# Output stages of a two-layer attention trunk: inverse sums loaded from DRAM as repeated rows, and the gates multiplied with them by GpSimd

## The reference

```
o     = attention output, still to be divided by the softmax sum of its head and token
mixed = (o / sum) * silu(gate)            # for A the factor is the RMS norm's inverse root instead
x     = x + mixed @ w_out                 # 1024 x 1024
out   = x * rsqrt(mean(x*x) + eps) * g    # the next layer's input, or the result
```

## Time and profile before

| | |
|---|---|
| runs, us | 2565.64, 2559.77, 2558.90 |
| median, us | 2559.77 |
| profiled execution, us | 2567.35 |
| its span, us | 2565.5 |
| mean granted TensorE clock | 0.973 |
| PE busy in the span | 2377.9 us, 93% |
| DVE, ACT, POOL busy | 60%, 44%, 42% |

### The profile page before, as it was taken

How to read it: one execution, slowest core, us unless ns; L and a number is a source line. 1 busy time by engine, 2 the same in 40 slices (tenths; PEclk the granted TensorE clock), 3 DMA queues, 4 the chain that set the end, 5 groups by cost and what they waited for, 6 DMA issues and landing times. The chain is left out here.

```text
span 2565.5 us, 46268 instructions
## 1 busy us (share of the span) xinstructions
PE 2377.9 (93%) x17864; PEld 1976.7 (77%) x17864; DVE 1528.9 (60%) x2849; ACT 1137.0 (44%) x2401; POOL 1072.4 (42%) x852
## 2 busy tenths in 40 slices
PE   5999999997999998799879999899997999998998
PEld 4777778875888877688768888788885888887887
DVE  6444565334988897855554423744223888887555
ACT  4333343333777776622143333433332666665221
POOL 6687758772000002401068877678774201000000
PEclk9999999998999999899989999999998999999999
DMA  3555434456663234757334444345434453533452
GB/s 130 169 177 177 152 118 149 148 176 149 136 145 88 63 115 132 215 199 261 131 130 158 160 126 141 99 156 170 126 103 146 147 178 129 189 130 112 165 196 83
DMA packets 220745, 376.76 MB, mean 147 GB/s; under 512 B 54980, under 2 KB 108912, under 8 KB 219504
## 3 DMA queue, kind: packets, MB, share of 16 engines
q1 hardware_dynamic: 199376, 296.21, 36.4%
q0 software_dynamic: 19792, 75.50, 10.0%
q10 hardware_dynamic: 1360, 2.10, 0.2%
HBM read 236.33 MB, written 142.90 MB: 148 GB/s over the span
## 5 line engine op out<-in xcount | busy, mean ns | idle before, releaser
L1092 PE MATMUL p_acc<-p_operands,p_w_hi 128*128 128x512 f32 x1600 | 613.5, 394 | 5.1 <-DVE p_full_out L959 4.9
L310 POOL TENSOR_TENSOR p_w_lo<-p_w_raw,p_w_hi 128x512 fp32r<-128x512 f32 x240 | 332.8, 1395 | 153.1 <-ACT p_w_hi L573 152.8
L1092 PE MATMUL p_acc<-share,p_w_hi 128*128 128x512 f32 x1024 | 385.2, 396 | 12.5 <-DVE p_operands L735 6.1
L1092 PEld LDWEIGHTS p_acc<-p_operands,p_w_hi 128*128 128x128 f32 x1600 | 303.6, 190 | 67.1 <-POOL p_w_raw L328 4.7
L1092 PE MATMUL p_acc<-share,p_w_lo 128*128 128x512 f32 x896 | 351.2, 392 | 0.0
L573 ACT ACTIVATE p_w_hi<-p_w_raw 128x512 fp32r<-128x512 f32 x252 | 156.5, 624 | 244.8 <-POOL p_w_raw L328 113.8
L1092 PE MATMUL p_acc<-share_low,p_w_hi 128*128 128x512 f32 x624 | 250.4, 401 | 12.5 <-DVE p_operands L735 6.1
L1092 PE MATMUL p_acc<-share_low,p_w_lo 128*128 128x512 f32 x624 | 246.1, 394 | 0.0
L1092 PEld LDWEIGHTS p_acc<-share,p_w_hi 128*128 128x128 f32 x1024 | 192.8, 189 | 54.9 <-DVE p_operands L735 8.9
L865 DVE SCALAR_TENSOR_TENSOR p_lo_out<-p_full_out,p_hi_out 128x512 fp32r<-128x512 f32 x116 | 123.1, 1061 | 180.3 <-ACT p_hi_out L590 180.3
L1850 DVE CUSTOM_DVE_ANT_0 c_prob<-c_logits,c_bias 128x640 f32<-128x640 f32 (+4 forms) x256 | 179.5, 738 | 68.8 <-PE c_logits L1783 52.6
(11 more groups left out here) (285 smaller groups left out, 4743.7 us busy)
## 6 DMA issues: line engine op xcount, KB each, us to landing
scr_qh<-p_hi_out SPq DMA_DIRECT2D x116, 256.0 KB, 2.5
scr_ql<-p_lo_out SPq DMA_DIRECT2D x116, 256.0 KB, 2.8
p_w_raw<-in_w_in_even POOLq DMA_DIRECT2D x26, 1024.0 KB, 7.5
scr_gt<-p_hi_out SPq DMA_DIRECT2D x128, 128.0 KB, 2.1
ready_w<-in_w_in_odd POOLq DMA_DIRECT2D x16, 1024.0 KB, 6.9
p_w_raw<-in_w_in_odd POOLq DMA_DIRECT2D x16, 1024.0 KB, 6.9
share<-scr_qh SPq DMA_DIRECT2D x28, 512.0 KB, 8.3
share<-scr_ql SPq DMA_DIRECT2D x28, 512.0 KB, 9.6
```

What stands on the lines that cost most here:

```text
L310: nc.gpsimd.tensor_tensor(w_lo[:, k, :, :], w_source(e, k), w_hi[:, k, :, :].bitcast(F32), ALU.subtract).then_inc(w_made, 1)
L1092: last = nc.tensor.matmul(bank[:, :], wt[:, k, c, :], at[k][:, c, :], start=starts and step == 0, stop=step == 3 * HK - 1, skip_group_chec ...
```

## The change

For tiles 0 and 1 the inverses come as before; tile 0 is done in two halves of 4 feature groups each (`pieces`), so that its first matmuls need only the first half. For tiles 2 to 15 there is no widening by POOL and no transposing by PE. Instead PE transposes the whole table of inverses once (`turn_inverses`, two products into PSUM `junk`), ACT copies it to SBUF (`inv_t`), SP stores it to a DRAM scratch `scr_inv` and waits until it has landed (`store_inverses`). Then SP loads each tile's rows from there, each row of 128 tokens repeated over 64 or 128 partitions by a zero stride of the source, into `post.wide` (`load_wide`). POOL multiplies the gates with `wide` (both in SBUF) into `gated`, once `mix` of the tile before is done. The loads of tiles 2 and 3 are issued ahead of the loop; that of tile t + 3 is issued in iteration t behind the load of x. DVE keeps `mix` and `m_lo`. Semaphore targets are raised by one for tile 0's second half (`after_tile(t)` is t + 2).

```diff
+        inv_rows = scr["inv"]
+        SPREADS = 2
+        rest = post.earlier
+        invs = [(post.inv_sums, min(post.heads, P // TILES) * h, min(post.heads, P // TILES)) for h in range(post.heads * TILES // P)]
+        if rest:
+            invs.append((rms, 0, rest))
+        WIDE_LOADS = 3 if rest else 2
+        HALVES = ((0, KC // 2), (KC // 2, KC))
...
         @block.gpsimd
...
-            for t in range(2, TILES):
-                pool.wait_ge(spread_done, t - 1)
-                post.widen(t, rms)
+            for t in range(SPREADS, TILES):
+                b = t // TPB
+                pool.wait_ge(wide_loaded[t % 2], 16 * WIDE_LOADS * (t // 2))
+                if b == 0:
+                    pool.wait_ge(post.tile_loaded[t], 32)
+                elif t % TPB == 0:
+                    pool.wait_ge(blk_loaded[b % 2], 32 * ((b + 1) // 2))
+                pool.wait_ge(mixed, after_tile(t - 1))
+                nc.gpsimd.tensor_tensor(gated[:, :, :], g_sb[b % 2][:, :, t % TPB * P:(t % TPB + 1) * P], post.wide[:, t % 2, :, :], ALU.mult).then_inc(scaled, 1)
...
         @block.sync
+            def store_inverses():
+                sp.wait_ge(inv_copied, len(invs))
+                for n, (source, first, heads) in enumerate(invs):
+                    sp.dma_start(inv_rows[n * P:n * P + heads * TILES, :], inv_t[0:heads * TILES, n, :]).then_inc(inv_stored, 16)
+                sp.wait_ge(inv_stored, 16 * len(invs))
+
+            def load_wide(t):
+                if t < 2 * SPREADS:
+                    sp.wait_ge(spread_done, t - 1)
+                else:
+                    sp.wait_ge(scaled, after_tile(t - 2))
+                for r in range(2):
+                    rows = bass.AP(tensor=inv_rows.tensor, offset=inv_rows.offset + (r * TILES + t) * P, ap=[[0, HD], [2 * TILES * P, KC - rest], [1, P]])
+                    sp.dma_start(post.wide[r * HD:(r + 1) * HD, t % 2, rest:KC, :], rows).then_inc(wide_loaded[t % 2], 16)
+                if rest:
+                    rows = bass.AP(tensor=inv_rows.tensor, offset=inv_rows.offset + (P + t) * P, ap=[[0, P], [TILES * P, rest], [1, P]])
+                    sp.dma_start(post.wide[:, t % 2, 0:rest, :], rows).then_inc(wide_loaded[t % 2], 16)
...
             sp.dma_start(gain[:, :], gain_dram.partition_broadcast(P)).then_inc(gain_loaded, 16)
+            store_inverses()
+            for t in range(SPREADS, 2 * SPREADS):
+                load_wide(t)
             for t in range(TILES):
                 if t + 2 < TILES:
                     load_x(t + 2)
+                if 2 * SPREADS <= t + 3 < TILES:
+                    load_wide(t + 3)
...
         @block.scalar
+            def high(t):
                 if t >= 2:
                     act.wait_ge(mm_done, 2 * (t - 1))
+                for n, (lo, hi) in enumerate(pieces(t)):
+                    act.wait_ge(mixed, n + 1 if t == 0 else after_tile(t))
+                    nc.scalar.activation(m_hi[:, t % 2, lo:hi, :], mix[:, lo:hi, :], ACT.Copy).then_inc(hi_done, 1)
+
+            high(0)
+            for n, (source, first, heads) in enumerate(invs):
+                act.wait_ge(inv_turned, n + 1)
+                nc.scalar.activation(inv_t[0:heads * TILES, n, :], junk[0:heads * TILES, n * BLK:n * BLK + P], ACT.Copy).then_inc(inv_copied, 1)
...
         @block.vector
-                dve.wait_ge(spread_done, t + 1)
-                nc.vector.tensor_tensor(gated[:, :, :].rearrange("p c (r t) -> p c r t", t=HD), g_sb[b % 2][:, :, tokens].rearrange("p c (r t) -> p c r t", t=HD),
-                                        spread_tokens, ALU.mult).then_inc(scaled, 1)
...
+                gate(0)
+                mixture(0)
+                if t == 0:
+                    gate(1)
+                low(0)
+                if t == 0:
+                    mixture(1)
+                    low(1)
...
         @block.tensor
             def spreads(t):
                 if t >= 1:
-                    pe.wait_ge(scaled, t)
+                    pe.wait_ge(scaled, after_tile(t - 1))
...
             spreads(0)
+            turn_inverses()
             for t in range(TILES):
-                if t + 1 < TILES:
+                if t + 1 < SPREADS:
                     spreads(t + 1)
-                pe.wait_ge(lo_done, t + 1)
+                if t >= 1:
+                    pe.wait_ge(lo_done, after_tile(t))
                 for half in range(2):
...
                     for c in range(KC):
+                        if t == 0 and half == 0 and c in (0, KC // 2):
+                            pe.wait_ge(lo_done, 1 if c == 0 else 2)
```

More of the change, by code:

```diff
@@ L2152, in output @@
         gated, mix = st.sb("gated", [P, KC, P]), st.sb("mix", [P, KC, P])
+        inv_t = st.sb("inv_t", [P, 2, P])
         x_sb = st.sb("x", [P, 2, D])
@@ L2162, in output @@
         spread_done, scaled = (st.sem(x) for x in ("spread_done", "scaled"))
+        inv_turned, inv_copied, inv_stored = (st.sem(x) for x in ("inv_turned", "inv_copied", "inv_stored"))
+        wide_loaded = st.sems("wide_loaded", 2)
         gain_loaded = st.sem("gain_loaded")
@@ L2168, in output, with pieces, after_tile @@
         gt = scr["gt"].rearrange("(c p) t -> p c t", p=P)
+        inv_rows = scr["inv"]
         x_v, y_v, n_v = (None if d is None else d.rearrange("(t p) d -> t p d", p=P) for d in (x_dram, y_dram, norm_dram))
+        SPREADS = 2
[5 more added lines that the diff above has]
+        HALVES = ((0, KC // 2), (KC // 2, KC))
+        def pieces(t):
+            return HALVES if t == 0 else ((0, KC),)
+        def after_tile(t):
+            return t + 2
         block = ctx.enter_context(nc.Block())
@@ L2218, in _ @@
         def _(act):
-            def hi(t):
-                act.wait_ge(mixed, t + 1)
+            def high(t):
                 if t >= 2:
                     act.wait_ge(mm_done, 2 * (t - 1))
-                nc.scalar.activation(m_hi[:, t % 2, :, :], mix[:, :, :], ACT.Copy).then_inc(hi_done, 1)
-            hi(0)
+                for n, (lo, hi) in enumerate(pieces(t)):
[5 more added lines that the diff above has]
+                nc.scalar.activation(inv_t[0:heads * TILES, n, :], junk[0:heads * TILES, n * BLK:n * BLK + P], ACT.Copy).then_inc(inv_copied, 1)
             for t in range(TILES):
                 if t + 1 < TILES:
-                    hi(t + 1)
+                    high(t + 1)
                 act.wait_ge(y_done, 2 * (t + 1))
@@ L2252, in split, with gate, mixture, low @@
                 tokens = slice(t % TPB * P, (t % TPB + 1) * P)
-                dve.wait_ge(spread_done, t + 1)
-                nc.vector.tensor_tensor(gated[:, :, :].rearrange("p c (r t) -> p c r t", t=HD), g_sb[b % 2][:, :, tokens].rearrange("p c (r t) -> p c r t", t=HD),
-                                        spread_tokens, ALU.mult).then_inc(scaled, 1)
[L2256 to L2259, removed]
+                if t < SPREADS:
+                    dve.wait_ge(spread_done, t + 1)
+                first = 1 if t == 0 else after_tile(t)
+                def gate(n):
+                    lo, hi = pieces(t)[n]
+                    if t < SPREADS:
+                        nc.vector.tensor_tensor(gated[:, lo:hi, :].rearrange("p c (r t) -> p c r t", t=HD), g_sb[b % 2][:, lo:hi, tokens].rearrange("p c (r t) -> p c r t", t=HD),
+                                                spread_tokens[:, lo:hi], ALU.mult).then_inc(scaled, 1)
+                def mixture(n):
+                    lo, hi = pieces(t)[n]
+                    dve.wait_ge(scaled, first + n)
+                    nc.vector.tensor_tensor(mix[:, lo:hi, :], o_sb[b % 2][:, lo:hi, tokens], gated[:, lo:hi, :], ALU.mult).then_inc(mixed, 1)
+                def low(n):
+                    lo, hi = pieces(t)[n]
+                    dve.wait_ge(hi_done, first + n)
+                    nc.vector.tensor_tensor(m_lo[:, t % 2, lo:hi, :], mix[:, lo:hi, :], m_hi[:, t % 2, lo:hi, :].bitcast(F32), ALU.subtract).then_inc(lo_done, 1)
+                gate(0)
[6 more added lines that the diff above has]
+                    low(1)
             split(0)
@@ L2295, in spreads, with turn_inverses @@
                 last.then_inc(spread_done, 1)
+            def turn_inverses():
+                for n, (source, first, heads) in enumerate(invs):
+                    nc.tensor.transpose(junk[0:heads * TILES, n * BLK:n * BLK + P], source[:, first:first + heads, :].rearrange("p h t -> p (h t)"),
+                                        keep["ident"][:, :]).then_inc(inv_turned, 1)
             spreads(0)
+            turn_inverses()
             for t in range(TILES):
-                if t + 1 < TILES:
+                if t + 1 < SPREADS:
                     spreads(t + 1)
-                pe.wait_ge(lo_done, t + 1)
+                if t >= 1:
+                    pe.wait_ge(lo_done, after_tile(t))
                 for half in range(2):
@@ L2327, in trunk @@
```

(2 more changed lines are left out.)

4 lines of the change are left out of this document (2 added, 2 removed).

## The result

| | before | after |
|---|---|---|
| median of the runs, us | 2561.88 (2558.9 to 2565.64, 4 runs) | 2669.22 (2667.86 to 2679.62, 4 runs) |
| ratio, 95% interval | | 1.0431 [1.0414, 1.0448] |
| span of the profiled execution | 2565.5 | 2666.1 |
| mean granted clock of TensorE | 0.973 | 0.959 |

The changed kernel takes 107 us more. The prediction was 2531.0, with a range up to 2546; the worst rival stood at 2575. It was wrong in sign and in size.

A forecast was written before the change was run, and what follows sets the result against it. The prediction took PE as the only bound in the steady part of the output stages. Transposes (24.1 us) plus first tile by halves (4.7) gave 28.8 us off 2559.8, so 2531.0 us, with a range of 2524 to 2546.

The forecast's parts named there:

- The wide loads: Per-tile loads of repeated inverse rows, 1.7 us at 307 GB/s, would fit the free DMA share and cost nothing.
- SP's queue: Wide loads put into SP's issue order would hold up nothing; each has 15.8 us to land.
- Transposes of tiles 2 to 15: In both output stages, 14 transposes each leave PE's path at 0.86 us apiece: 24.1 us off.
- First tile by halves: At both stage starts, first matmuls begin about 3.3 us after the first gated: 4.7 us off (2.5 to 8.8).
- the low stretch: First matmuls after PE's idling run at half clock; tile 0 takes 13.18 instead of 11.11 us, assumed unchanged.
- Gates on POOL: POOL's gate multiplication, 2.38 us a tile, stays hidden, m_lo taking between 1.2 and 2.5 us: no cost.
- DMA share of 0.93 in four tiles of o0: Sign to look for: busy DMA share in o0 with the wide loads added, (32.8 + 7.8)/43.6.
- The sum: Whole kernel: 24.1 us for transposes plus 4.7 us for the first tile, 28.8 us off.
- The wide loads cost four times their price: Rival: in o0, loads take 7.8 units a tile, 44 us more, giving 2575; chance 0.07.
- The wide loads are heavy in o0: Rival: a load costs 5.1 units, 11 us in o0, full effect in o1, giving 2542; chance 0.09.
- DVE becomes the bound: Rival: POOL's 2.38 us fall on DVE's work, cycle 11.07 us, 5 us lost, giving 2536; chance 0.08.
- nothing is gained: Rival: loads land late at 17.5 us, tiles stay at 11.75 us, giving 2557 to 2560; chance 0.06.

The follow-up runs named there:

- near: Load-only form with the repeated 512-byte rows side by side instead of 16 KB apart: nearly as fast as rows 16.5 KB apart.
- pitch: Load-only form with the changed kernel's repeated rows 16.5 KB apart instead of 16 KB: 4.1 us against 11.2.
- m1: Kernel of DMAs alone, layers' computation left out, 0.5 MB per step from ten source patterns: 11.2 us as in the change, 4.0 with each partition's own rows.
- e5: Changed kernel with a head's table rows 17 rows apart instead of 16, stored by small transfers: 2542.79 us, ratio 0.9936 to the kernel before.
- e1: Changed kernel, wide loads reading each partition's own rows of the gates array, scaling left out: 2537.16 us, ratio 0.9908 to the kernel before.
- e4: Changed kernel, slow table kept, without the wide loads of tiles 4 to 15: 2563.11 us, ratio 1.0013 to the kernel before.
- e6: Changed kernel with a tile's table rows side by side and a block's two 2 MB parts issued in two tiles: 2538.55 us, ratio 0.9919.
- e8: The kernel of e6 run once more, in more rounds: 2537.85 us, ratio 0.9915 to the kernel before.
- e3: Kernel before with only its first tile by halves, DVE's gates and all transposes kept: 2557.08 us, ratio 0.9985.
- m2: Second kernel of DMAs alone, eight transfers (2.1 MB) a step at several row pitches: 34.3 us at 16 KB, 11.3 at 16.5 KB.
- e7: e6 with a block's parts issued behind the stores of y and n instead of ahead of them: 2549.34 us, ratio 0.996 to the kernel before.

## Why the prediction was wrong, step by step

**The step that failed is "The wide loads".** It took nothing, from two rows of busy stretches at 307 and 283 GB/s, and said that "repetition by itself costs nothing visible". The sentence is true (near and pitch in m1), but each of the two rows had one of two traits, and only both together cost. The first block's rows of 512 bytes lie 8 KB apart (2048 tokens of 4 bytes), but each is read once. Skewing reads each row 128 times, but its rows lie 383 x 4 bytes, 1.5 KB, apart. The table has 16 rows of 512 bytes a head, so the eight rows that one half of the partitions reads are 16 KB apart, and each is read 64 times. Measured, a tile's load runs at 45 GB/s and takes about 12 us instead of 1.7, seven times the price. That the pitch of the repeated rows is the cause is shown by m1 (alone, 11.2 against 4.1 us) and by e5 (in the kernel, 126 us); that the pitch without the repetition is harmless, by m1's own (4.0 us) and e1 (5.3 us).

**The step "SP's queue" failed with it.** It allowed a load 15.8 us to land; in the changed kernel the loads landed at 16.8 us at the median, with POOL waiting up to 24.4. It also counted only 1.7 us of SP's time for the new packets; with wide loads at 45 GB/s ahead of it, a store of y lands after 18.0 us and the next tile's buffers come late. e4 puts a size to it: with two slow loads a stage it is 25 to 26 us above e6 and e1 in the medians (2563.11 against 2538.55 and 2537.16), though it has twelve loads a stage fewer, and PE's waits for m_lo in it are 24.6 us.

**The other steps, read from e1, e4, e6 and e8, where the loads are not slow:**

- *Transposes of tiles 2 to 15, 24.1 us.* Right in mechanism, a little large. A tile takes 10.96 us without them, not 10.89, so each is worth 0.79 us and all 28 are worth 22.1. The traces agree: from the 48th matmul (the end of tile 0) to the last n, o0 of e1 is 11.1 us shorter than before, 14 x 0.79; o1 is 9.9 shorter, with 1.6 us of waiting for m_lo in it.
- *First tile by halves, 4.7 us.* The first matmul starts 3.1 us after the first gated, in both stages of the changed kernel (predicted 3.3). What the start is worth came out larger. From the first gated to the 48th matmul's start, before took 18.4 and 18.1 us, the changed kernel 14.9 and 14.9. That is 6.8 us saved over the two stages; in e1 and e6 it is 5.9 and 5.8. The prediction kept the low stretch as long as it was. In o0 before it is 3.9 us of matmuls 0.43 us apart, and 2.2 in the changed kernel; what shortened it was not tested. Alone, in e3, the term is only 3.5 us in the trace and 3.0 in the medians: POOL's copies still ran beside it (mix by halves took 1.04 and m_lo 0.87 us in o0 instead of 0.69), and the low stretch stayed at 3.9.
- *Gates on POOL, nothing.* Right while the loads are in time: 2.39 us at the median (predicted 2.38), and in e4 PE does not wait for twelve tiles. The bound of 2.5 us for m_lo was too low: in e6 it reaches 3.41, where the gate, released late by a load, begins with m_lo and not with m_hi (timeline of e6: start, us, what):

```profile
2447.36 2.39 POOL L2204 TENSOR_TENSOR o_gated<-share,post_wide 128x1024 f32<-128x1024 f32 x1 [8.44 <-DMA post_wide<-scr_inv]
...
2447.42 3.41 DVE L2324 TENSOR_TENSOR o_m_lo<-o_mix,o_m_hi 128x1024 fp32r<-128x1024 f32 x1 [1.19 <-ACT o_m_hi L2273]
```

  The Trainium skill, SBUF — State Buffer, section Who interferes with whom, calls it a lock that the first comer holds for its whole instruction. By that rule m_lo would take the last 2.33 us of the gate and then its own 1.23, 3.56 in all; the measured 3.41 is near it. In the earlier trace rows the size agreed, but not the order: mix starts 0.17 us ahead of the copy beside which it is longer.
- *DMA share of 0.93 in four tiles of o0.* Near: 0.95, 0.67, 0.98, 0.86 and 0.84 in five stretches of 25 us of e6, 0.86 in the mean. So the room for the bytes was there.
- *The sum.* 28.8 predicted, 22.5 to 22.9 measured in the medians of e8 and e1. In e6's trace the two stages are 25.2 us shorter than before: the start gives 5.8 where 4.7 was taken, the transposes 22.1 where 24.1 was taken, and PE's waits for m_lo behind POOL's gates, which were taken as nothing, cost 3.1, in the tiles where a block arrives. These make 24.8. The other 2.6 us, between trace and medians, stay open; the profiled execution of before took 2567.35 us, 5.5 above its median.

**The rivals.** "The wide loads cost four times their price" had the right sign and named the right suspicion (all engines read the same few rows), at 0.07. Its price was too small: it let only o0 suffer, since o1 has more free share. But the load ran at 45 GB/s whatever share was busy, and o1 lost 45 us too. The counter-argument (skewing) should not have stood: its repeated rows lie 1.5 KB apart, not 16. "The wide loads are heavy in o0" is refuted by o1, which was to keep its full gain. "DVE becomes the bound" is refuted by e4, "nothing is gained" by the size, though its mechanism, PE waiting for late loads, is what the chain shows.

## What to carry to other kernels

Before a load is priced by bytes, write down the DRAM addresses that its requests touch at one time, and how often each is read. If a small table is read over and over, keep its rows off the pitches that were slow here, 8, 16 and 32 KB; one row of padding (16.5 KB) was enough. Rows at such a pitch that are read once were fast. Price a new transfer by a row whose source has the same pattern in both traits, and where the trace has none, give a wide bound and take it as the main risk. A slow transfer in a shared queue also delays those behind it.

## What the runs showed of the hardware

- Repeated reads of 512-byte rows at pitches of 8, 16 and 32 KB ran at 61 to 71 GB/s (m2, eight transfers of 64 partitions), reads of one row at 37 GB/s (13.8 ns each); the same bytes at 0.5 to 2 KB or 16.5 KB ran at 169 to 186 GB/s.
- Rows 16 KB apart that were read once ran at 172 GB/s (m2), so pitch or repetition alone was not slow.
- The busy share of the DMA engines is no measure of what they move: in the changed kernel it rose from 0.2 to 1.0 at a constant 45 GB/s, and in m2 the reads of one row ran at 37 GB/s with a share of 0.2.
- PE waits of 1.9 to 2.4 us, three in o0 of e7, went with a granted clock of 0.93 to 0.98 where e6, with waits of at most 0.8 us there, had 1.00.
- A DVE operation of 1.23 us alone took 3.41 us when a POOL operation of 2.39 us had begun 0.06 us before it (e6).
